# A hybrid decoder trunk on one core: a new table of slots for the second mixer's end and for the routing

## The chip, the cores and the metric

The kernel runs on one core of one Trainium2 chip. The metric is the device time of one launch in microseconds (us), the median of three runs. A profiled execution of the same program gives the trace; its times are of that one execution.

## What is computed

Two residual layers on a stream x of 256 tokens by 1024 features, all in float32. The tokens are handled as two blocks of 128.

```python
for layer in range(2):
    hn = rmsnorm(h, attn_norm[layer])
    h = h + (pool_attention_mixer(hn, ...) if layer == 0 else ssd_mixer(hn, ...))
    h = h + peer_ffn(rmsnorm(h, ffn_norm[layer]), ...)

def block(xb):                                   # peer_ffn, for 128 tokens
    q = (xb @ w_q).reshape(n, 8, 2, 128)
    s = einsum('nhie,ike->nhik', q, keys)
    top_s, top_i = top_k(s, 16)                  # then the 16 best of the 16 x 16 sums
    gate = softmax(best_s)
    act = gelu(einsum('nhkd,nd->nhk', expert_u[idx], xb))
    return einsum('nhk,nhkd->nd', gate * act, expert_v[idx])
```

Each token thus picks 8 heads x 16 = 128 of 16384 experts, each with one row of u and one of v, 4 KiB each. Gathering these rows is most of the data that is moved: 2 layers x 2 blocks x 128 picks x 1 MiB.

## The kernel before

The kernel goes through four phases (layer 0 block 0, layer 0 block 1, layer 1 block 0, layer 1 block 1) of 128 slots. In a slot, one pick of each of the 128 tokens is handled. POOL gathers u and v of the 128 rows (1 MiB, line 437) into one of ten places of `ring`; VectorE multiplies u by hn and sums it (`dot`, line 1305); ScalarE takes the gelu (line 907); VectorE multiplies by the gate (`coefs`, line 1313); ScalarE makes a diagonal matrix of each coefficient (line 914); TensorE multiplies it with v and adds up in `acc` (line 752). The last four go by pairs of slots. POOL issues the gather of a slot ten slots on only when the pair that used its place has been summed on TensorE (`pairs_summed`).

Beside these slots, every engine works in its own program order on the mixer and the queries of the *next* phase (`side`), and on the routing of the heads (`route`: top 16, candidates, expert numbers, gate). Each of these is a Python generator that yields *ticks*; each engine runs its steps up to the tick that `pace(phase, n)` gives for slot n. `pace` interpolates linearly between the `KNOTS`, which come from the table `SIDE_SLOTS`. In the second mixer `T_IN1` begins the input projection, `T_CB` and `T_SCAN` the chunked scan, `T_YT` the transposes of y, `T_OUT1` the output projection (four weight chunks of 2 MiB, 16 ticks), whose two halves VectorE adds to h in `add_to_stream` (an operation recorded at line 963, `h<-h,dve_bank`); at `T_END1` VectorE does the norm for the queries (`prepare`), and from `T_END1 + T_Q` each head's queries take four ticks. The side program of a phase starts at slot 4 (`FIRST_SIDE`) of the phase before (14 in phase 0). So table slot 81, say, is slot 85 of the phase. In slots 2 and 3 of phases 1 to 3, VectorE adds the sums of the phase before to h (`add_even`, `add_odd`), and at slot 4 begins the next norm. TensorE's pair sums stand two slots behind in its program (it sums the pair 2, 3 while VectorE is meant to be at slot 5).

SyncE loads the weight chunks into two buffers, each as soon as TensorE has used the last one. The routing of a head has four parts, at the slots in `ROUTE_DUE`: part 0 the top 16 of both score rows, part 1 the candidates, part 2 the expert numbers (after which POOL may gather for the head), part 3 the gate.

In this, the order on each engine is fixed when the program is built: an engine that waits holds up everything behind it.

Of the kernel before, what the change touches and what calls it, by code (L numbers as in the profile page):

```python
# [13 lines left out]
NBLK = SEQ // P  # L14
# [16 lines left out]
PH, NK, HALF, TOPK = 8, 128, 128, 16  # L31
# [5 lines left out]
SLOTS = PH * TOPK  # L37
# [25 lines left out]
T_SCAN = T_CB + 6  # L63
T_YT = T_SCAN + 30
T_OUT1 = T_YT + 4
T_END1 = T_OUT1 + 16 + 1
T_END = (T_END0, T_END1)
T_Q, T_PART = 3, 4
T_QUERIES = T_Q + T_PART * PH
# [3 lines left out]
START = [0]  # L73
for _phase in range(PHASES):
# [1 line left out]
EARLY_HEADS = 4  # L76
T_EARLY = T_END0 + T_Q + T_PART * EARLY_HEADS - 1
QUERIED_BY = 14
ASKED_BY = 121

HALF_P = P // 2
AHEAD = RING // GROUP
# [3 lines left out]
    ((0, 0.5), (3, 1), (5, 2), (6, T_IN0), (32, T_IN0 + 16), (56, T_OUT0), (70, T_OUT0 + 8), (72, T_END0),  # L86
     (74, T_END0 + 1), (76, T_END0 + 2), (77, T_END0 + T_Q)),
    ((0, 0.5), (3, 1), (5, 2), (6, T_IN1 - 2), (9, T_IN1 - 1), (10, T_IN1), (40, T_IN1 + 32), (46, T_CB), (51, T_SCAN),
     (73, T_YT), (76, T_YT + 1), (77, T_YT + 2), (80, T_YT + 3), (81, T_OUT1), (93, T_OUT1 + 16), (94, T_END1),
     (96, T_END1 + 1), (98, T_END1 + 2), (99, T_END1 + T_Q)),  # L90
)
FIRST_SIDE = GROUP + 2
KNOTS = [(0, T_EARLY + 1), (QUERIED_BY - 1, START[1])]
for _phase in range(1, PHASES):
    _from = (_phase - 1) * SLOTS + (QUERIED_BY if _phase == 1 else FIRST_SIDE)
    for _slot, _tick in SIDE_SLOTS[_phase // NBLK]:
        KNOTS.append((_from + _slot, START[_phase] + _tick))
    KNOTS.append(((_phase - 1) * SLOTS + ASKED_BY, START[_phase + 1]))
    KNOTS.append((_phase * SLOTS, START[_phase + 1]))


ROUTE_PARTS = 4
ROUTE_LEAD, ROUTE_STEP = 20, 3
ROUTE_DUE = []
for _phase in range(PHASES):
    for _head in range(PH):
# [45 lines left out]
def build_trunk(nc, io):  # L152
# [6 lines left out]
    with ctx:  # L159
# [193 lines left out]
        def pace(phase, n):  # L353

            return float(np.interp(phase * SLOTS + n, *zip(*KNOTS)))

        def routes_due(phase, n):

            return sum(due <= phase * SLOTS + n for due in ROUTE_DUE) - 1

        def one_after_another(side):

            for phase in range(PHASES):
                yield START[phase] + 0.5
                for tick in side(*divmod(phase, NBLK)):
                    yield START[phase] + tick
# [416 lines left out]
        def _(act):  # L783
# [120 lines left out]
            def take_gelu(g, q):  # L904
                cols = slice(q * GROUP, (q + 1) * GROUP)
                act.wait_ge(sem("dot_done"), g * BODY + (q + 1) * GROUP)
                act.activation(acts[:, cols], dots[:, cols], ACT.Gelu).then_inc(sem("gelu_done"), 1)  # L907

            def make_diagonals(g, q):
                act.wait_ge(sem("coef_done"), g * GROUPS + (q + 1))  # L910
                for rows in range(2):
                    act.wait_ge(sem(f"pairs_summed{rows}"), g * GROUPS + (q + 1 + AHEAD - DIAGS // GROUP))
                for s in range(GROUP):
                    ins = act.activation(diag[:, (q * GROUP + s) % DIAGS], folded, ACT.Copy,  # L914
                                         scale=coefs[:, q * GROUP + s:q * GROUP + s + 1])
                ins.then_inc(sem("diag_ready"), 1)
# [14 lines left out]
            def experts(phase, beside, routes):  # L931
                first = phase * STEPS
                for n in range(SLOTS):
                    g, q = first + n // BODY, n % BODY // GROUP
                    if n % GROUP == GROUP - 1:
                        take_gelu(g, q)
                    if n >= FIRST_SIDE or not phase:
                        beside.upto(pace(phase, n))
                    routes.upto(routes_due(phase, n))
                    if n % GROUP == GROUP - 1:  # L940
                        make_diagonals(g, q)
                    if n == GROUP - 1 and phase:
                        copy_odd(phase - 1)
# [4 lines left out]
            beside, routes = Side(one_after_another(side)), Side(all_routes(route))  # L948
# [9 lines left out]
        def _(dve):  # L958
# [121 lines left out]
            def mixer1(b):  # L1080
# [122 lines left out]
                    tt(yT[:, 4 * c:4 * c + 4], banks_in.take().rearrange("p (k t) -> p k t", k=4),  # L1203
                       gate_gain[:, 4 * c:4 * c + 4].unsqueeze(2).to_broadcast([P, 4, P]), name="dve_emptied")
                for n in range(2):
                    yield T_OUT1 + 8 * n + 8
                    add_to_stream(b, n, banks_in.take(), "dve_emptied")

            def top16(*rows):
# [137 lines left out]
            def experts(phase, beside, routes):  # L1347
                first = phase * STEPS
                for n in range(SLOTS):
                    g = first + n // BODY  # L1350
                    dot(phase, g, n % BODY)
                    if n == GROUP and phase:
                        add_even(phase - 1)
                    if n == GROUP + 1 and phase:
                        add_odd(phase - 1)
                        if phase == PHASES - 1:
                            lane.tell("out_ready")
                    if n >= FIRST_SIDE or not phase:
                        beside.upto(pace(phase, n))
                    routes.upto(routes_due(phase, n))  # L1360
                    if n % GROUP == GROUP - 1:
                        coefficients(phase, g, n % BODY // GROUP)

            dve.wait_ge(sem("x_loaded0"), 16)
            beside, routes = Side(one_after_another(side)), Side(all_routes(route))
# [58 lines left out]
```

## Time and profile before

| what | value |
|---|---|
| median of three runs | 1685.33 us (1685.25 to 1685.48) |
| the profiled execution | 1688.61 us |
| its span in the trace | 1686.8 us |
| TensorE matmul, VectorE, ScalarE, POOL busy | 1200.5, 1186.6, 496.0, 579.5 us |
| moved by the DMA engines | 670.19 MB, mean 397 GB/s |
| expert gathers, weight chunks | 512 of 1 MiB, 60 of 2 MiB |

Phase 0 starts near 106 us, phase 1 near 498, phase 2 near 930, phase 3 near 1353 us of the span (the first dots of each). Busy time of TensorE is modelled and overlaps; GB/s is what the core's 16 DMA engines moved in a stretch. In the rows, `<-` names what an engine waited for just before the operation.

### The profile page before, as it was taken

How to read it: one execution, taken by the hardware profiler on the slowest of the kernel's cores; microseconds unless marked ns; L12 is line 12 of the kernel's file. 1: busy time of each engine (PE TensorE's matmuls, PEld its weight loads, DVE VectorE, ACT ScalarE, POOL GpSimd, SP SyncE). 2: the span in 40 equal slices, each digit the busy share in tenths (PEclk: the TensorE clock that was granted, in tenths of full speed). 3: DMA queues.
4: the chain of work that ended last, by engine and by line, in shares of the span. 5: the costliest groups of instructions: out<-in, count | busy, mean ns of one | idle time of the engine just before them, and what ended most of it. 6: DMA issues, size and time to landing. Idle time of an engine off the chain costs nothing.

```text
span 1686.8 us, 21750 instructions
## 1 busy us (share of the span) xinstructions
PE 1200.5 (71%) x7384; PEld 578.5 (34%) x7384; DVE 1186.6 (70%) x3380; ACT 496.0 (29%) x1139; POOL 579.5 (34%) x525
## 2 busy tenths in 40 slices
PE   6866876767857985886786698589687855566554
PEld 2453222224423653442253266344234511111111
DVE  3355768866568877888574888788937587777754
ACT  0121224312222543462122354255202322222211
POOL 1023423433334322323233433232323444444551
PEclk9987988888977997998999699899798977767787
DMA  8579999999999999999999999999999999999995
GB/s 306 194 290 423 422 423 421 390 424 421 423 422 406 425 422 406 367 397 386 424 415 422 412 423 423 422 418 393 372 404 387 421 422 421 422 421 421 422 420 240
DMA packets 84076, 670.19 MB, mean 397 GB/s; under 512 B 9376, under 2 KB 9520, under 8 KB 10624
## 3 DMA queue, kind: packets, MB, share of 16 engines
q0 software_dynamic: 74608, 540.65, 78.0%
q1 hardware_dynamic: 9216, 127.65, 18.2%
q8 instruction: 58, 0.95, 0.2%
q10 hardware_dynamic: 144, 0.52, 0.1%
q14 instruction: 50, 0.41, 0.1%
HBM read 667.74 MB, written 1.05 MB: 396 GB/s over the span
## 4 chain that ended last, share of the span: by engine, by line
DMA 30%; PE 28%; DVE 28%; issue 6%; ACT 6%; POOL 1%; DVEq 0%; POOLq 0%; SPq 0%; ACTq 0%; PEldq 0%
DMA ring<-in_experts,idx 28%; PE acc L752 13%; DVE ring L1305 9%; PE act_bank L494 6%; PE dve_bank L480 5%; DVE scratch L963 3%; DMA wbuf<-in_weights 3%; ACT L788 2%; DVE onehot L963 2%; DVE scratch L1119 1%; ACT diag L914 1%; POOL ring L437 1%; ACT scratch L788 1%; PE act_bank L480 1%; PE act_bank L733 1%
## 5 line engine op out<-in xcount | busy, mean ns | idle before, releaser
L437 POOL DMA_INDIRECT ring<-in_experts,idx x512 | 573.4, 1120 | 1060.0 <-PE acc L752 864.3
L752 PE MATMUL acc<-ring,diag 64*64 64x512 f32 x4096 | 624.4, 738 | 377.5 <-ACT diag L914 366.6
L1305 DVE CUSTOM_DVE_ANT_0 ring<-ring,hn 128x1024 f32<-128x1024 f32 x512 | 621.3, 1223 | 227.5 <-DMA ring<-in_experts,idx 210.7
L752 PEld LDWEIGHTS acc<-ring,diag 64*64 64x64 f32 x4096 | 156.1, 156 | 744.7 <-ACT diag L914 497.8
L494 PEld LDWEIGHTS act_bank<-hnT,wbuf 128*128 128x128 f32 x2048 | 238.9, 194 | 63.6 <-issue 62.0
L494 PE MATMUL act_bank<-hnT,wbuf 128*128 128x128 f32 x2048 | 253.0, 281 | 10.8 <-ACT scratch L788 9.6
L907 ACT ACTIVATE acts<-dots 128x2 f32<-128x2 f32 x256 | 52.0, 203 | 709.3 <-DVE dots L1305 708.1
L914 ACT ACTIVATE diag<-cst,coefs 128x64 f32<-128x64 f32 x512 | 150.3, 340 | 262.8 <-DVE coefs L1313 250.6
L788 ACT ACT_TABLE_LOAD x80 | 102.6, 1283 | 11.7 <-DMA rowc<-in_rows 9.2
L1313 DVE TENSOR_TENSOR coefs<-acts,gate 128x2 f32<-128x2 f32 x256 | 41.3, 161 | 87.6 <-ACT acts L907 78.7
L480 PE MATMUL dve_bank<-wbuf,scratch 128*128 128x512 f32 x192 | 93.7, 627 | 8.6 <-DMA wbuf<-in_weights 7.3
L907 ACT ACT_TABLE_LOAD x68 | 87.2, 1283 | 7.3 <-DVE dots L1305 1.2
L788 ACT ACTIVATE scratch<-act_bank 128x512 f32<-128x512 f32 (+2 forms) x94 | 48.0, 511 | 132.6 <-PE act_bank L494 80.1
L681 PE MATMUL act_bank<-wbuf,hnT 128*128 128x512 f32 x128 | 59.0, 598 | 0.0
L480 PEld LDWEIGHTS dve_bank<-wbuf,scratch 128*128 128x128 f32 x192 | 35.3, 197 | 68.5 <-issue 62.9
L963 DVE TENSOR_TENSOR h<-h,dve_bank 128x512 f32<-128x512 f32 x8 | 5.5, 688 | 67.9 <-PE dve_bank L480 67.9
L1119 DVE SCALAR_TENSOR_TENSOR scratch<-scratch,colc 128x128 f32<-128x128 f32 x192 | 53.1, 346 | 0.0
L733 PE MATMUL act_bank<-keysT,scratch 128*128 128x128 f32 x128 | 23.5, 310 | 34.8 <-issue 26.4
L1305 DVE DVE_READ_ACCUMULATOR2_ANT dots<- 128x1 f32 x512 | 42.3, 83 | 0.0
L963 DVE TENSOR_TENSOR scratch<-scratch 128x512 f32<-128x512 f32 (+3 forms) x45 | 34.8, 774 | 10.2 <-ACTq L316 7.4
L480 PE MATMUL act_bank<-wbuf,hnT 128*128 128x512 f32 x64 | 33.8, 670 | 4.6 <-DMA wbuf<-in_weights 4.0
L480 PE MATMUL dve_bank<-wbuf,hnT 128*128 128x512 f32 x64 | 32.7, 654 | 3.7 <-DVE hnT L963 2.4
(128 smaller groups left out, 823.4 us busy)
## 6 DMA issues: line engine op xcount, KB each, us to landing
wbuf<-in_weights SPq DMA_DIRECT2D x60, 2048.0 KB, 11.9
ring<-in_experts,idx POOLq DMA_INDIRECT x512, 15.6
scratch<-in_bias POOLq DMA_DIRECT2D x1, 1024.0 KB, 11.3
out<-h SPq DMA_DIRECT2D x2, 512.0 KB, 5.3
scratch<-in_bands POOLq DMA_DIRECT2D x1, 768.0 KB, 6.5
h<-in_x SPq DMA_DIRECT2D x1, 512.0 KB, 4.4
gains<-in_gains POOLq DMA_DIRECT2D x1, 512.0 KB, 4.6
h<-in_x POOLq DMA_DIRECT2D x1, 512.0 KB, 17.5
```

What stands on the lines that cost most here:

```text
L437: pool.indirect_dma_start(ring[:, n % RING], None, io[f"experts{layer}"], bass.IndirectOffsetOnAxis(idx[:, at:at + 1], 0),).then_inc(sem(f ...
L480: ins = pe.matmul(out[:, 0:cols], lhsT[:, k], w[:, k], start=first and k == 0, stop=last and k == KD - 1)
L494: ins = pe.matmul(out[:, n * P:(n + 1) * P], w[:, k, j * P:(j + 1) * P], hnT[:, k], start=k == 0, stop=k == KD - 1)
L681: ins = pe.matmul(out_z, hnT[:, k], w[:, k], start=k == 0, stop=k == KD - 1)
L752: last[rows] = pe.matmul(acc[rows][half][home:home + HALF_P], diag[part, n % DIAGS], ring[part, slot, D + half * CW:D + (half + 1) * CW], ...
L788: lane(act.activation(out, in_, func, **more), name)
L907: act.activation(acts[:, cols], dots[:, cols], ACT.Gelu).then_inc(sem("gelu_done"), 1)
L914: ins = act.activation(diag[:, (q * GROUP + s) % DIAGS], folded, ACT.Copy, scale=coefs[:, q * GROUP + s:q * GROUP + s + 1])
L963: lane(dve.tensor_tensor(out, in0, in1, op), name)
L1119: done = lane.start(dve.scalar_tensor_tensor(out, tiles[:, j, tap:tap + P], taps[:, t, tap:tap + 1], out, ALU.mult, ALU.add))
L1305: dve.tensor_tensor_reduce(out=ring[:, slot, 0:D], in0=ring[:, slot, 0:D], in1=hn[:, phase % NBLK], scale=1.0, scalar=0.0, op0=ALU.mult, o ...
L1313: dve.tensor_tensor(coefs[:, cols], acts[:, cols], gate[:, bass.ds(at, GROUP)], ALU.mult).then_inc(sem("coef_done"), 1)
```

## The change

The table of slots is changed in four places, and nothing else: no operation is added or taken away.

1. The second mixer's output product takes 15 slots in place of 12, the scan's last steps and the transposes stand up to one slot from where they were, and each half of the product is added to h three ticks later (`T_OUT1 + 8n + 11`). `T_END1` is three ticks later to fit; in slots the norm for the queries moves from 94 to 101 of the table, the first query from 99 to 106.
2. The last queries are asked by other slots (`LAST_ASKED`): those for phase 2 by slot 132, four slots into phase 2; those for phase 3 two heads by slot 118 of phase 2, and the other six spread up to slot 80 of phase 3.
3. A head's routing begins 14 slots ahead of its first slot in place of 20, with 2 slots between its four parts in place of 3.
4. ScalarE and VectorE may do side steps in the first four slots of a phase too.

```diff
-T_END1 = T_OUT1 + 16 + 1
+T_END1 = T_OUT1 + 16 + 4
...
-ASKED_BY = 121
...
-     (73, T_YT), (76, T_YT + 1), (77, T_YT + 2), (80, T_YT + 3), (81, T_OUT1), (93, T_OUT1 + 16), (94, T_END1),
-     (96, T_END1 + 1), (98, T_END1 + 2), (99, T_END1 + T_Q)),
+     (70, T_SCAN + 27), (72, T_SCAN + 29), (74, T_YT), (77, T_YT + 1), (78, T_YT + 2), (81, T_YT + 3), (82, T_OUT1),
+     (97, T_OUT1 + 16), (101, T_END1), (103, T_END1 + 1), (105, T_END1 + 2), (106, T_END1 + T_Q)),
 )
+LAST_ASKED = {1: ((121, PH),), 2: ((SLOTS + 4, PH),), 3: ((118, 2), (SLOTS + 80, PH))}
...
-    KNOTS.append(((_phase - 1) * SLOTS + ASKED_BY, START[_phase + 1]))
-    KNOTS.append((_phase * SLOTS, START[_phase + 1]))
+    for _slot, _heads in LAST_ASKED[_phase]:
+        KNOTS.append(((_phase - 1) * SLOTS + _slot, START[_phase] + T_END[_phase // NBLK] + T_Q + T_PART * _heads))
...
-ROUTE_LEAD, ROUTE_STEP = 20, 3
+ROUTE_LEAD, ROUTE_STEP = 14, 2
...
-                    if n >= FIRST_SIDE or not phase:
-                        beside.upto(pace(phase, n))
+                    beside.upto(pace(phase, n))
...
-                    yield T_OUT1 + 8 * n + 8
+                    yield T_OUT1 + 8 * n + 11
```

The guard is taken out on ScalarE and on VectorE alike; TensorE had none.

## Rows read from the trace of the kernel before

**Rows 1.** The page, transfers in 40 equal slices of the span, GB/s.

```profile
GB/s 306 194 290 423 422 423 421 390 424 421 423 422 406 425 422 406 367 397 386 424 415 422 412 423 423 422 418 393 372 404 387 421 422 421 422 421 421 422 420 240
```

**Rows 2.** Windows by phase: busy us of each engine, PEclk, DMA share, GB/s.

```profile
120.00:500.00 380.00, 271.34 (x1624) 119.28 (x1627) 264.73 (x742) 100.19 (x263) 137.95 (x126) 0.85 1.01 419
500.00:927.00 427.00, 330.06 (x2184) 180.77 (x2176) 317.04 (x920) 153.98 (x314) 138.60 (x126) 0.91 0.99 407
927.00:1353.00 426.00, 331.82 (x2192) 181.46 (x2188) 328.80 (x958) 153.03 (x314) 141.55 (x130) 0.90 0.99 408
1353.00:1665.00 312.00, 175.29 (x996) 43.29 (x1000) 219.22 (x591) 71.41 (x213) 145.31 (x121) 0.75 1.01 421
```

**Rows 3.** Who waited for whom: us in total, times, longest us.

```profile
DVE h L963 <- PE dve_bank L480: 67.9, 7, 13.7
```

**Rows 4.** Timeline of VectorE: start us, us, operation, idle before and its releaser.

```profile
833.55 0.69 DVE L963 TENSOR_TENSOR h<-h,dve_bank 128x512 f32<-128x512 f32 x1 [9.84 <-PE dve_bank L480]
...
1239.70 0.69 DVE L963 TENSOR_TENSOR h<-h,dve_bank 128x512 f32<-128x512 f32 x1 [13.75 <-PE dve_bank L480]
...
1266.16 0.69 DVE L963 TENSOR_TENSOR h<-h,dve_bank 128x512 f32<-128x512 f32 x1 [12.85 <-PE dve_bank L480]
```

**Rows 5.** Windows around the output product of phases 1 and 2, columns as above.

```profile
780.00:860.00 80.00, 61.83 (x303) 24.33 (x296) 50.30 (x134) 15.15 (x44) 26.42 (x24) 0.89 1.00 407
1210.00:1300.00 90.00, 70.64 (x352) 30.18 (x352) 54.43 (x157) 16.61 (x50) 25.87 (x26) 0.89 0.97 394
```

**Rows 6.** Timeline of TensorE in the output product of phase 2.

```profile
1214.41 3.69 PE L752 MATMUL acc<-ring,diag 64*64 64x512 f32 x16 [4.55 <-ACT diag L914]
...
1222.68 1.95 PE L752 MATMUL acc<-ring,diag 64*64 64x512 f32 x16
1224.56 5.80 PE L480 MATMUL dve_bank<-wbuf,scratch 128*128 128x512 f32 x12
```

**Rows 7.** Timeline of VectorE: a landing awaited; first and following instruction of routing parts.

```profile
501.10 1.23 DVE L1305 CUSTOM_DVE_ANT_0 ring<-ring,hn 128x1024 f32<-128x1024 f32 x1 [0.68 <-DMA ring<-in_experts,idx]
...
505.23 0.17 DVE L1255 TENSOR_SCALAR pos_hi<-best_pos 128x16 uint32<-128x16 uint32 x1
...
509.00 1.23 DVE L1305 CUSTOM_DVE_ANT_0 ring<-ring,hn 128x1024 f32<-128x1024 f32 x1 [0.19 <-DVE idx L1274]
...
518.25 0.17 DVE L1292 TENSOR_REDUCE stat<-expd 128x1 f32<-128x16 f32 x1
...
518.93 0.16 DVE L1313 TENSOR_TENSOR coefs<-acts,gate 128x2 f32<-128x2 f32 x1
...
1241.64 0.48 DVE L1213 MAX8 top_s<-scores 128x8 f32<-128x128 f32 x2
...
1244.26 1.23 DVE L1305 CUSTOM_DVE_ANT_0 ring<-ring,hn 128x1024 f32<-128x1024 f32 x1 [0.18 <-DVE top_i L1217]
...
1248.13 0.29 DVE L1246 TENSOR_TENSOR cand<-top_s 128x128 f32<-128x128 f32 x1
...
1250.86 0.16 DVE L1313 TENSOR_TENSOR coefs<-acts,gate 128x2 f32<-128x2 f32 x1
```

**Rows 8.** Timeline of POOL: gathers (the first of each pair).

```profile
524.31 0.94 POOL L437 DMA_INDIRECT ring<-in_experts,idx  x1 [4.82 <-PE acc L752]
...
527.39 1.65 POOL L437 DMA_INDIRECT ring<-in_experts,idx  x1 [0.89 <-PE acc L752]
...
531.17 0.94 POOL L437 DMA_INDIRECT ring<-in_experts,idx  x1 [0.56 <-issue]
...
1204.13 0.94 POOL L437 DMA_INDIRECT ring<-in_experts,idx  x1 [9.45 <-PE acc L752]
```

**Rows 9.** Windows of 5 us where the transfers dip, columns as above.

```profile
525.00:530.00 5.00, 5.00 (x48) 2.83 (x44) 4.66 (x12) 1.38 (x5) 3.50 (x4) 1.00 0.87 329
955.00:960.00 5.00, 5.00 (x35) 2.16 (x28) 4.43 (x8) 1.15 (x5) 1.88 (x2) 0.77 0.95 362
1200.00:1205.00 5.00, 4.53 (x28) 1.01 (x24) 4.61 (x18) 0.79 (x3) 0.87 (x1) 0.70 0.49 205
```

More of the change, by code:

```diff
@@ L1357, in experts @@
                             lane.tell("out_ready")
-                    if n >= FIRST_SIDE or not phase:
-                        beside.upto(pace(phase, n))
+                    beside.upto(pace(phase, n))
                     routes.upto(routes_due(phase, n))
```

## The prediction, made before the changed kernel was run

> **What bounds the kernel now.** I read the page first, its line of GB/s above all. From the fourth slice on the transfers run at about 422 GB/s, with dips [rows 1]; no compute engine is near full, TensorE busy 330 and VectorE 317 of the 427 us of phase 1 [rows 2]. So the DMA engines bound the kernel, and a compute engine counts only where it lets them run dry. The second view is the windows by phase [rows 2]. Against the 421 of the last phase, taken as 422 at full flow, the lost time is 380 x 3/422 = 2.7 us in phase 0, 427 x 15/422 = 15.2 in phase 1, 426 x 14/422 = 14.0 in phase 2, and 312 x 1/422 = 0.7 in phase 3: 32.6 us between 120 and 1665. The bytes are the same after the change, and the start and the tail are untouched, so no version of this table can give more than about 33 us, and each part is to be priced as dry time of the DMA engines.
>
> A slot's gather is 1 MiB, 1.049 MB / 422 GB/s = 2.49 us; a pair of slots takes 4.98, and so, nearly, does a 2 MiB weight chunk (4.97). The ring holds ten slots: the gather of slot n+10 is issued when TensorE has summed slot n. A late VectorE or TensorE is thus free until the queue of gathers is empty.
>
> The third view is who waits: VectorE waits 67.9 us, 7 times, for the output product before it adds it to h [rows 3]. Two such waits stand in each block of the second mixer, four in all, three of which are shown, of 9.8 to 13.75 us [rows 4]. They are at slots 91 and 97 of phases 1 and 2. But 50 us of waits aren't 50 us of time: the windows around them show what they and the late norm behind them cost, 80 x 15/422 = 2.8 us in phase 1 and 90 x 28/422 = 6.0 us in phase 2 [rows 5].
>
> **The change, part by part.** *Output of the second mixer and the end.* The four chunks of the output product are spread over 15 slots in place of 12, and each half's add comes three ticks later. TensorE's work: 12 matmuls take 5.80 us, so a chunk of 16 takes 7.7 and four take 31; a pair's sum takes 1.9 at full clock [rows 6]. In 12 slots that is 31 + 6 x 1.9 = 42 us, while the gathers of 12 slots take 30 and the two or three chunks that load meanwhile take 10 to 15: TensorE is level with the supply or behind it. In 15 slots it is 31 + 7.5 x 1.9 = 45 against 37 + 15 = 52. The first add came 6 slots after the product's first tick, with TensorE finished at 5.3 slots plus the two by which its sums trail; now it comes 10.3 slots after it, with TensorE at 6.6 plus two. The wait should go from 13 us to nearly none. The norm behind it moves from slot 98, where it stood beside the stall and the third part of a routing, to 105. What is recovered lies between 0 and 8.8 us (2.8 + 6.0); I take 8.0, since the sums above leave TensorE room and nothing else is late there. What is late next is the first routing of the next block, due at slot 114, one slot after ScalarE's copy of its scores; were it missed, VectorE would wait about a slot, 2.5 us, under a queue of gathers.
>
> *Routing 14 slots ahead, in steps of 2.* Nothing is added; the four parts of each head move from slots 12, 15, 2 and 5 (modulo 16) to 2, 4, 6 and 8. They take VectorE 2.6 us (part 0), 2.7 (part 1), 3.8 (part 2) and 0.7 (part 3) [rows 7]. Indices come out at the slot whose number is 8 below the head's first; gathers run at most ten ahead of the sums, and slot 7's pair is coefficients and a sum later than part 2 at slot 6, so POOL gets no new wait. The cost lies at the start of phases 1 and 2. There VectorE does the adds of the last phase (slots 2 and 3) and the next norm (slots 4 and 5). In slots 0 to 2 VectorE is level with the landings (it waits 0.68 us for one at 501.10 [rows 7]), and still will be. Counted from there, route work done before: 3.8 by slot 3, 4.5 by slot 5, and no more to slot 9. After: 2.6, 5.3, 9.1 by slot 7, 9.8 by slot 9. So the sums of slots 4/5, 6/7 and 8/9 come 0.9, 4.6 and 5.3 us later. Before, the gathers they release start at 524.31, 527.39 and 531.17 [rows 8], and the DMA engines run partly dry just then (5 x (1 - 329/422) = 1.1 us in one window) [rows 9]. After: 525.2, 532.0, 536.5. The first costs 0.9; the next gap is 6.8 where one pair feeds only 4.98, which costs 1.8 to 1.9; the next gap, 4.5, costs nothing. That is 2.8 us. In phase 2 the pattern repeats with a dip of 0.7 us [rows 9]; I take 2.8 again, 5.6 in all. Phase 3 has no norm there and showed no dry time; I take 0, with 5.3 as the other end.
>
> *Scan of the second mixer.* Its steps move by at most one slot. Dry time there comes from VectorE's sum of work up to slot 77: the gather that ends the largest gap (2.6 us in one window) starts at 1204.13, right after the pair 76/77 [rows 8, 9]. From slot 42 to 77 it does 22.2 us of routing before (nine parts) and 19.6 after (eight): a gain of 2.6, if it enters slot 42 no later. It enters later, by up to 5.3 us, as the parts of slots 34 to 40 come later; waits for landings there swallow some of it. Per block that is +2.6 to -2.7; I take +0.5, 1.0 in all.
>
> *Phase 0.* Only the routings move. Its 2.7 us of dry time fall where the first mixer's attention and output meet routing parts, now out of slots 60 and 63. Between -1 and +2.7; I take 1.0.
>
> *Queries.* Six heads of the last block go to phase 3, slots 0 to 80, and phase 1's end runs to slot 132. The bytes are the same; TensorE is busy 175 of 312 us in phase 3 and VectorE 219 [rows 2]. The queries of a head come some 17 slots ahead of its routing. Nothing, then; without that cover, a head late by a slot would cost 2.5. Letting side steps run in slots 0 to 3 touches just these queries: 0.
>
> Sum: 8.0 + 1.0 + 1.0 - 5.6 + 0 = 4.4 us less. The profiled execution took 1688.6 (span 1686.8 and 1.8 around it), and would take 1684.2; the median of the runs is 3.3 lower, 1685.3, and so 1680.9.
>
> **The rivals.** (1) *The stalls were cover.* Half the loss around them stays, because TensorE's sums, not VectorE, set the gathers' pace there: 4.0 in place of 8.0, thus 1684.9. For it: 13 us waits cost only 2.8 us in phase 1. Against: the spreading helps TensorE too. (2) *Packed routing costs more than the output gives.* All three phase starts lose the whole 5.3 us: 16 us, against 10.0 of gains: 1691.3, slower. It decides where the gather released by slots 6/7 starts over 4.98 us after the one before it with an empty queue. For it: phases 1 and 2 were already at that edge. Against: the ring has cover in phase 3, and the parts formerly at slots 124 and 127 are gone. (3) *The scan gains as well.* If VectorE enters slot 42 on time and half the 15.2 + 14.0 of phases 1 and 2 goes: 14.6 + 1 - 5.6 = 10.0 less, 1675.3. (4) *TensorE cools in the thinned product.* The 16 matmuls of a sum sometimes take 3.69 us in place of 1.95 [rows 6], which I read as the lower of the two levels, 1.2 GHz; a chunk would go from 7.7 to some 14.6, the block's stretch from 45 to 86 against a supply of 52. The gathers would fall short by up to 34 us in each of two blocks; if half of that came true, 1685.3 + 34 is about 1719. But TensorE would then be busy throughout, and busy stretches here hold the full clock. The Trainium skill, TensorE: Matmul & The Clock Gate, section "HAM oscillation — how this bites in real kernels", has thinly fed TensorE falling back to half rate; the mean clock of 0.75 in phase 3, where TensorE is least busy, agrees [rows 2].
>
> **How the numbers follow.** Forecast 0.49, its own range 1677 to 1682. Rival 1: 0.26. Rival 2: 0.13. Rival 3: 0.10. Rival 4: 0.02. Two tenths of a per cent are 3.4 us, about what a measurement of this kernel can tell from no change: faster means under 1681.9. The forecast and rival 3 give faster 0.59, rival 1 same, 0.26, rivals 2 and 4 slower, 0.15. The range from 1673.0 to 1688.0 leaves out rivals 2 and 4 and the far end of rival 3, just under 2 in 10.
>
> **What would show it.** Right: VectorE's waits before h<-h,dve_bank at slots near 97 and 104 under 4 us; about 420 GB/s through that stretch in phases 1 and 2. Right on the cost: some 30 us after the starts of phases 1 and 2 the GB/s dip by 2 to 3 us more each than the 1.1 and 0.7 of before. Wrong: gather gaps in the output stretch stay at 6 us and more (rival 1); phase 3 below 421 GB/s at its start (rival 2); no gap near slot 86 of phase 2 (rival 3). The whole is wrong if dry time appears at a place not named here, such as slots 66 to 77, where routing now meets the scan.

## The result, and the profile after

The changed kernel was slower: median 1692.0 us of five runs (1688.6 to 1694.7) beside 1685.3 for the kernel before, run on the same chip; the ratio is 1.0035, 95% interval 1.0021 to 1.0049. A second series of 12 runs gave 1691.8 and 1.0029 [1.0016, 1.0043]. Forecast was 1680.9, with 1673 to 1688 as the range. Ratios here come with their 95% intervals; they differ by up to 0.0015 (in e1) from the plain quotient of the medians.

The profiled execution of the changed kernel took 1688.6 us, the fastest of its five, and that of the kernel before 1688.6 too, 3.3 above its median. So the two traces can show where time moves, but their totals don't show the difference; that comes from the runs. Part of it is the start: the first dot of phase 0 stands at 106.4 us of the span before, and at 102.8 in the changed kernel, 3.6 us earlier (104.2 in the trace of its second series).

The first view is the page's line of transfers in 40 slices, beside [rows 1]:

```profile
GB/s 306 199 315 422 425 420 409 401 422 421 423 422 380 423 424 422 352 414 363 426 419 422 417 424 424 421 380 413 327 424 422 421 421 423 421 420 422 421 421 241
```

Slices are 42.2 us. Slices 30 and 31, where the output product of phase 2 stands, are full (424 and 422; before 404 and 387). Dips have become deeper at slice 13 (406 to 380, the start of phase 1), 17 (367 to 352), 19 (386 to 363), 27 (418 to 380) and 29 (372 to 327). Slices 3 (290 to 315), 18 (397 to 414) and 28 (393 to 413) are fuller, partly because a phase now starts 5 to 11 us earlier in the span, so that the same slice holds other slots. The same in windows, columns as in [rows 2]:

```profile
500.00:545.00 45.00, 30.71 (x206) 14.93 (x207) 39.53 (x125) 13.41 (x32) 17.89 (x14) 0.78 0.97 382
925.00:975.00 50.00, 34.82 (x226) 21.73 (x225) 39.39 (x113) 18.29 (x43) 17.31 (x16) 0.80 1.01 417
690.00:705.00 15.00, 14.69 (x71) 7.26 (x64) 10.20 (x27) 9.85 (x14) 4.03 (x4) 0.89 0.66 234
755.00:775.00 20.00, 12.58 (x76) 4.75 (x76) 17.67 (x42) 5.43 (x15) 6.97 (x6) 0.74 0.78 289
1120.00:1135.00 15.00, 12.99 (x67) 7.38 (x67) 10.75 (x25) 9.85 (x14) 4.88 (x4) 1.00 0.80 304
1175.00:1210.00 35.00, 20.96 (x116) 8.32 (x116) 31.14 (x76) 10.21 (x22) 11.06 (x9) 0.80 0.79 295
780.00:860.00 80.00, 56.14 (x248) 18.18 (x248) 53.51 (x157) 15.04 (x42) 28.22 (x25) 0.85 1.01 423
1210.00:1300.00 90.00, 67.75 (x311) 23.14 (x312) 62.76 (x182) 18.41 (x52) 30.11 (x30) 0.83 1.01 423
1353.00:1665.00 312.00, 185.25 (x1156) 63.91 (x1156) 218.92 (x609) 71.69 (x217) 145.07 (x118) 0.81 1.01 421
```

- The two output windows are at 423, where they were at 407 and 394 [rows 5].
- The end of the scan is where the time went: 1175 to 1210 at 295 GB/s is 35 x (1 - 295/422) = 10.5 us of lost flow. The same windows of the kernel before, for phase 2:

```profile
1120.00:1135.00 15.00, 14.34 (x75) 7.33 (x76) 13.13 (x43) 10.77 (x17) 4.91 (x5) 1.00 1.02 419
1175.00:1210.00 35.00, 23.40 (x138) 9.41 (x137) 32.65 (x96) 12.91 (x26) 13.92 (x12) 0.80 0.86 345
```

Before it was 35 x (1 - 345/422) = 6.4 there. VectorE is busy 31.1 of the 35 us (32.7 before), while the transfers are far from full: in this stretch the DMA engines wait for the compute engines.

Who waits, columns as in [rows 3]:

```profile
DVE ring L1304 <- DMA ring<-in_experts,idx: 267.5, 191, 7.3
DVE h L962 <- PE dve_bank L480: 17.3, 2, 10.6
DVE scratch L1152 <- PE dve_bank L652: 5.9, 3, 2.6
DVE scratch L962 <- PE dve_bank L664: 3.0, 2, 2.3
```

Of the 67.9 us before `h`, 17.3 are left, all in the first mixer: the four waits of the second mixer are gone. VectorE waits for landings instead (267.5 us in the first line, 210.7 before), which costs nothing while the transfers are at full flow. The last two lines are the scan's own (decay product and group product on TensorE, awaited by VectorE); the kernel before had 2.7 and 1.0 there.

POOL's gathers at the end of the scan of phase 2, beside the last row of [rows 8]:

```profile
1189.15 1.20 POOL L437 DMA_INDIRECT ring<-in_experts,idx  x1 [11.14 <-PE acc L752]
...
1193.99 1.29 POOL L437 DMA_INDIRECT ring<-in_experts,idx  x1 [1.53 <-PE acc L752]
...
1205.43 0.94 POOL L437 DMA_INDIRECT ring<-in_experts,idx  x1 [8.17 <-PE acc L752]
```

Two gaps, of 11.1 and 8.2 us, where a pair of slots feeds the engines for 5; before there was one such gap, of 9.45. What VectorE does in them is the timeline of some of its work there (the dots between are left out):

```profile
1152.15 0.42 DVE L962 TENSOR_TENSOR scratch<-dve_bank,scratch 128x256 f32<-128x256 f32 x1 [2.27 <-PE dve_bank L664]
...
1154.74 2.36 DVE L962 TENSOR_TENSOR scratch<-scratch 128x512 f32<-128x512 f32 x3
...
1157.86 0.49 DVE L1212 MAX8 top_s<-scores 128x8 f32<-128x128 f32 x2
...
1174.42 2.37 DVE L962 TENSOR_TENSOR scratch<-scratch 128x512 f32<-128x512 f32 x3 [0.32 <-ACTq L316]
...
1177.54 0.17 DVE L1254 TENSOR_SCALAR pos_hi<-best_pos 128x16 uint32<-128x16 uint32 x1
```

A scan group's arithmetic (in the first case a wait of 2.27, then 2.36 for its three wide operations) and a routing part stand close together: part 0 at 1157.86, part 2 at 1177.54.

**Dry time by slots.** Windows in us don't follow the same work from kernel to kernel, so I also counted by slots: the time between the dots of two slots, less the bytes moved meanwhile over 422.5 GB/s. In each column the first number is phase 1, the second phase 2, in us; the last column is the median of the runs. It is arithmetic on the traces, one execution each, good to about 1 us an entry; e12 is the changed kernel a second time, e15 is e5 a second time, and the other labels are explained below.

```
slots             0-14      14-42     42-60     60-80      80-104    104-128    sum  median
before            1.7  1.0  -0.1 -0.1  4.4  0.2  5.2  4.1  3.5  6.9  0.8  2.7   30.2  1685.3
changed           2.7  0.0   1.4  0.4  3.9  1.0  8.8 12.9  1.1  0.5  0.2  0.4   33.3  1692.0
e12_changed       2.5  0.0   1.3  0.2  2.0  1.1  8.4 14.5  1.2  0.9  0.2  0.3   32.6  1691.8
e1_route_only     3.6  4.1   1.3  0.9  3.8  0.4  5.9  8.0  0.6  3.6  0.2  0.4   32.6  1688.0
e2_heads_back     1.6  0.1  -0.2  0.0  4.7  1.8  8.2 10.5  3.0  2.4  0.2  0.3   32.7  1688.7
e3_old_scan       2.5  0.1   1.1  0.3  3.1  0.1  4.4  7.0  2.8  3.7  0.1  0.1   25.3  1684.4
e5_output_only    3.1  0.3  -0.2 -0.1  4.9  2.0  4.7  3.0  2.7  4.4 -0.1  0.2   24.8  1681.6
e15_output_again  1.4  0.1  -0.1 -0.1  4.6  1.8  4.7  4.9  2.4  4.4  0.1  0.2   24.4  1683.7
e6_norm_early     3.2  0.0   0.2  1.2  1.8  0.5  4.7 11.5  0.9  2.2  0.1  0.3   26.7  1685.2
e7_squeezed       3.4  0.1   0.1  0.0  1.6  1.3  6.0 11.8  3.6  3.0  0.1  0.3   31.1  1690.3
e8_add_late       1.2  1.7   0.0 -0.2  5.1  0.4  6.2  3.7  2.9  6.2  0.0  0.2   27.3  1684.2
e14_packed_early  0.2  0.1   0.0  0.2  5.6  4.0  4.1  3.5  4.6  5.4  0.1  0.3   28.2  1688.4
```

Slots 80 to 128 fell from 13.9 to 2.1 us, 11.8 less, more than the 8.0 forecast for the output. Not all of it is the output's: without its edit, e1 has 4.7 there, 9.2 less than before, and with its edit alone e15 has 7.1, 6.8 less. Slots 60 to 80 rose from 9.3 to 21.7, 12.4 more, 10.3 of it in slots 74 to 80 (1.9 to 12.2).

### The profile page after: what moved, and what is told of

The parts are those of the page before. It is cut to its first block, busy times and chain, and to the rows that moved or that the text cites. A ratio compares the mean times of both kernels' runs of the same rounds, so it can differ in the third digit from the quotient of the medians.

```text
span 1686.8 us, 21747 instructions
## 1 busy us (share of the span) xinstructions
PE 1203.2 (71%) x7384; PEld 591.5 (35%) x7384; DVE 1191.1 (71%) x3380; ACT 489.5 (29%) x1135; POOL 602.0 (36%) x525
## 4 chain that ended last, share of the span: by engine, by line
DVE 33%; DMA 29%; PE 24%; issue 6%; ACT 4%; POOL 1%; DVEq 0%; POOLq 0%; SPq 0%; ACTq 0%; PEldq 0%
DMA ring<-in_experts,idx 27%; DVE ring L1304 12%; PE acc L752 10%; PE act_bank L494 6%; PE dve_bank L480 4%; DVE scratch L962 3%; DMA wbuf<-in_weights 3%; DVE onehot L962 2%; POOL ring L437 1%; ACT L788 1%; PE act_bank L681 1%; DVE scratch L1118 1%; PE act_bank L480 1%; ACT scratch L788 1%; ACT diag L914 1%
## 5 line engine op out<-in xcount | busy, mean ns | idle before, releaser
L437 POOL DMA_INDIRECT ring<-in_experts,idx x512 | 596.0, 1164 | 1037.7 <-PE acc L752 851.0
L752 PE MATMUL acc<-ring,diag 64*64 64x512 f32 x4096 | 603.5, 714 | 358.6 <-ACT diag L914 343.1
L1304 DVE CUSTOM_DVE_ANT_0 ring<-ring,hn 128x1024 f32<-128x1024 f32 x512 | 624.6, 1224 | 287.4 <-DMA ring<-in_experts,idx 267.5
L752 PEld LDWEIGHTS acc<-ring,diag 64*64 64x64 f32 x4096 | 151.5, 151 | 690.2 <-ACT diag L914 448.9
L494 PE MATMUL act_bank<-hnT,wbuf 128*128 128x128 f32 x2048 | 268.2, 290 | 21.9 <-ACT scratch L788 13.9
L494 PEld LDWEIGHTS act_bank<-hnT,wbuf 128*128 128x128 f32 x2048 | 252.3, 203 | 86.5 <-issue 79.2
L733 PE MATMUL act_bank<-keysT,scratch 128*128 128x128 f32 x128 | 25.3, 327 | 39.7 <-issue 34.6
L733 PEld LDWEIGHTS act_bank<-keysT,scratch 128*128 128x128 f32 x128 | 19.3, 216 | 56.7 <-issue 56.7
```

What stands on the lines that cost most here:

```text
L437: pool.indirect_dma_start(ring[:, n % RING], None, io[f"experts{layer}"], bass.IndirectOffsetOnAxis(idx[:, at:at + 1], 0),).then_inc(sem(f ...
L494: ins = pe.matmul(out[:, n * P:(n + 1) * P], w[:, k, j * P:(j + 1) * P], hnT[:, k], start=k == 0, stop=k == KD - 1)
L733: ins = pe.matmul(out[:, i * NK:(i + 1) * NK], qT[:, 2 * hd + i], keysT[:, layer, i], start=True, stop=True)
L752: last[rows] = pe.matmul(acc[rows][half][home:home + HALF_P], diag[part, n % DIAGS], ring[part, slot, D + half * CW:D + (half + 1) * CW], ...
L1304: dve.tensor_tensor_reduce(out=ring[:, slot, 0:D], in0=ring[:, slot, 0:D], in1=hn[:, phase % NBLK], scale=1.0, scalar=0.0, op0=ALU.mult, o ...
```

## The experiments

Every kernel was run beside the kernel before on the same chip, and the ratios are to that. All edits are to the changed kernel unless it says "from the kernel before".

### Which part costs

The theory: two costs that add up, the scan's moved steps (the larger) and the packed routing, against a gain at the output as forecast. The rival: a single overload at slots 60 to 80 that only the meeting of both makes, so that undoing either gives back all.

**e1_route_only**, from the kernel before:

```diff
-ROUTE_LEAD, ROUTE_STEP = 20, 3
+ROUTE_LEAD, ROUTE_STEP = 14, 2
```

> The kernel before, with only the routing changed to 14 slots ahead in steps of 2. Theory R (the routing's new place costs, because its four parts now fall on slots 66 to 72, on top of the scan of the second mixer, and on slots 2 to 8, on top of the adds and the norm): the dips at 690 to 705, 755 to 775, 1125 to 1135 and 1175 to 1210 us that the changed kernel shows are here too, and the output stretch still loses its 8.8 us: 1693 to 1701. Rival S (the scan's and the transposes' new slots, with queries in the first slots, made the dips): no new dips, 1684 to 1688.

Measured: 1688.0 us, 1.0002 [0.9986, 1.0018], far below what theory R gave. The new dips of the scan are there in part (273, 401, 345 and 360 GB/s in the four scan windows above, where the changed kernel has 234, 289, 304 and 295). And the output stretch doesn't still lose its 8.8 us, though the product and the adds stand as before:

```profile
780.00:860.00 80.00, 61.14 (x290) 24.19 (x291) 53.57 (x157) 16.15 (x44) 27.10 (x24) 0.91 1.01 423
1210.00:1300.00 90.00, 70.48 (x366) 29.31 (x363) 60.27 (x179) 18.25 (x51) 30.88 (x28) 0.91 0.99 408
```

The four waits before `h` fell from 49.7 to 30.2 us. So the routing edit alone moves dry time rather than adding much: by the slots 7.3 us more up to slot 42, 4.2 more from 42 to 80, 9.2 less from 80 on. The start of phase 2, for which the changed kernel is at 417 and the kernel before at 414:

```profile
925.00:975.00 50.00, 30.33 (x183) 11.59 (x179) 40.85 (x113) 16.56 (x39) 19.46 (x16) 0.73 0.95 379
```

That is 50 x (414 - 379)/422 = 4.1 us more there (3.1 by the slots 0 to 14 in the count, and 1.9 in phase 1). The phase-start loss exists in both phases. In the changed kernel phase 2's is absent. My reading is that a weight chunk fills the hole, since its last queries now run to slot 132; no run changes that alone. SyncE's timeline of the changed kernel has two loads between 905 and 960 us, 23.7 us from the first's issue to the end of the second's, thus the second near 940:

```profile
916.82 23.68 SPq L385 DMA_DIRECT2D wbuf<-in_weights  x2
```

The kernel before and e1 have one load there, at 905.50 and 906.01.

**e2_heads_back**, routing of all heads but the first as before. (The first head of a phase can't go back to 20 slots ahead: its top 16 would stand at slot 108 of the phase before, and its queries are asked from slot 110. That wasn't tried.)

```diff
-            _due = _phase * SLOTS + _head * TOPK - ROUTE_LEAD + _part * ROUTE_STEP
+            _due = _phase * SLOTS + _head * TOPK - (20 - 3 * _part if _head else ROUTE_LEAD - _part * ROUTE_STEP)
```

> The changed kernel, with the old routing (20 ahead, steps of 3) for heads 1 to 7; only head 0 of each block keeps 14 ahead in steps of 2, as its scores aren't there earlier. Theory R: the output product's gain stays and the scan's dips go back to the size of before: 1674 to 1681, faster than both kernels. Rival S: the dips stay, 1689 to 1694.

Measured: 1688.7, 1.0012 [1.0000, 1.0024]: not faster than both kernels, so theory R missed, and the dips of slots 60 to 80 stayed (18.7 us).

**e3_old_scan**, the scan's steps as before, everything behind it as changed:

```diff
-     (70, T_SCAN + 27), (72, T_SCAN + 29), (74, T_YT), (77, T_YT + 1), ...
+     (73, T_YT), (77, T_YT + 1), ...
```

> The changed kernel, with the scan's ticks up to the transposes spread evenly over slots 51 to 73 as before (the transposes and the output keep their new slots). Theory R: the sum of VectorE's work up to slot 77 is the same, so within 3 us of the changed kernel, 1689 to 1695. Rival S: the dips at 1175 to 1210 shrink by half or more, 1680 to 1686.

Measured: 1684.4, 0.9994 [0.9976, 1.0013], as rival S had it. Three of the windows shown above:

```profile
755.00:775.00 20.00, 13.91 (x90) 5.33 (x93) 18.82 (x45) 5.50 (x16) 8.55 (x9) 0.83 1.00 412
1120.00:1135.00 15.00, 14.85 (x79) 7.47 (x78) 10.78 (x26) 10.52 (x15) 5.13 (x5) 1.00 0.88 346
1175.00:1210.00 35.00, 23.04 (x140) 8.76 (x143) 32.46 (x86) 11.69 (x26) 15.23 (x13) 0.90 0.95 360
```

They were 289, 304 and 295. One edit of three knots moves these by (412 - 289) x 20/422 = 5.8, 1.5 and 35 x 65/422 = 5.4 us. By the slots, 60 to 80 has 11.4 us in place of 21.7.

**e4_no_spread**, all the last queries by slot 4 of phase 3:

```diff
-LAST_ASKED = {..., 3: ((118, 2), (SLOTS + 80, PH))}
+LAST_ASKED = {..., 3: ((SLOTS + 4, PH),)}
```

> The changed kernel, with the last block's queries not spread over the last phase but asked by slot 4 of it, as the phase before does. Theory R: nothing but the place of one 2 MiB weight load changes, 1690 to 1694. A rival that blames the last phase (queries late, a cooler TensorE): 1684 to 1688, and GB/s of the last phase goes up from its 421.

Measured: 1692.7, 1.0043 [1.0029, 1.0058], beside 1.0035 and 1.0029 of the changed kernel. By the middle values the place of the last block's queries is worth 1.3 or 2.4 us, and the intervals overlap: no effect that these runs show.

**e5_output_only** has the edits of e2 and e3 together; **e15_output_again** is the same kernel a second time.

> The changed kernel with both the old scan spacing and the old routing of heads 1 to 7, that is, the output product's room, the late adds and the spread queries alone. Theory T (three parts that add up: the output gives about 9 us back, the scan's new spacing costs about 7, the routing's new place about 3): 1692 - 7.6 - 3.3 = 1681, between 1678 and 1683. Rival U (time that VectorE doesn't lose at the output is lost at the scan in any case, since transfers only run dry later): 1684 to 1688.

> The kernel of e5_output_only again, beside the other two on one chip: 1680 to 1683 and faster than the kernel before by 0.2 to 0.4 per cent.

Measured: 1681.6, 0.9967 [0.9953, 0.9981], of six runs; again, of eleven, 1683.7, 0.9980 [0.9969, 0.9990]. This is the version that beats both kernels, as theory T had it.

What follows, in ratios (means of the two series where there are two):

```
                   routing 14 / 2       routing as before
scan as changed    1.0032 (changed)     1.0012 (e2)
scan as before     0.9994 (e3)          0.9974 (e5, e15)
```

The scan's knots cost 0.0038 in the one column and 0.0038 in the other, 6.4 us; the packed routing 0.0020 in both rows, 3.4 us; what is left is -0.0026, 4.5 us less. These two effects add, and the single overload falls: undoing either gives back only its own share. The intervals are 0.0010 to 0.0018 to each side, so a difference of two ratios is known to some 0.002. The scan's cost is clear of that, the routing's isn't, and with the output as before (e1) it is 0.0002. By the quotients of the medians the scan costs 0.0041 and 0.0040, the routing 0.0016 and 0.0015 (0.0017 in e1), and what is left is -0.0020, 3.3 us less: the same picture, with less at the output. The dry time agrees on the scan (7.6 us in the one column, 8.1 in the other, by the means of the traces) and shows only 0.3 and 0.7 us for the routing. Whether output and routing add as well isn't shown. The count speaks against it: both edits clear slots 80 to 128, where e1 has 4.7 us and e15 7.1 of the 13.9, and what one has cleared the other can't gain.

### Why the scan's knots cost 6 us

The old line from (51, `T_SCAN`) to (73, `T_YT`) does 1.36 ticks a slot, and so reaches tick 27 after 19.8 slots. The new knots do 27 ticks in 19 slots, 1.42 a slot, then slow down: ticks 27 to 30 come by slot 70, 71, 72 and 74. Two things are mixed in that: the squeezed steps, and the early normalization behind tick 29. One run has each alone.

**e6_norm_early**, the old rate up to tick 27, then early:

```diff
-     (70, T_SCAN + 27), (72, T_SCAN + 29), (74, T_YT), ...
+     (70.8, T_SCAN + 27), (71, T_SCAN + 28), (72, T_SCAN + 29), (74, T_YT), ...
```

> The changed kernel, scan steps at their old slots, only y's normalization (ticks 28 and 29, 5.7 us of VectorE) one slot earlier, at 75 and 76 as in the change. Theory V (the scan's cost comes from rounding of the squeezed ticks to slots: VectorE's group sum falls into the slot of TensorE's product that it needs, three waits of 2 to 3 us a block): near the old spacing, 1683 to 1687. Rival W (the cost is the normalization, which is now due before the pair of slots 74 and 75 can be summed): 1689 to 1693.

Measured: 1685.2, 0.9999 [0.9987, 1.0010]: 0.0005 above e3, 0.8 us, within the noise, and as theory V had it. One entry speaks against it: its slots 60 to 80 of phase 2 are 11.5 us dry (7.0 in e3), though phase 1 has 4.7 (4.4), its slots 80 to 128 are 3.2 us less dry, and the sum over all slots is 26.7 (25.3).

**e7_squeezed**, the new rate up to tick 27, then late:

```diff
-     (70, T_SCAN + 27), (72, T_SCAN + 29), (74, T_YT), ...
+     (70, T_SCAN + 27), (71.5, T_SCAN + 28), (72.25, T_SCAN + 29), (74, T_YT), ...
```

> The reverse: the changed kernel's squeezed scan steps, with the normalization at its old slots 76 and 77. Theory V: 1689 to 1693, with VectorE's waits for the group products at slots 62 to 65 as in the changed kernel. Rival W: 1683 to 1687.

Measured: 1690.3, 1.0025 [1.0016, 1.0035], which is 0.0031 above e3, 5.2 us, and 0.0026 above e6, which ran on the same chip; those two intervals lie apart. Its waits in the scan:

```profile
DVE scratch L1152 <- PE dve_bank L652: 7.4, 3, 4.1
DVE scratch L962 <- PE dve_bank L664: 3.0, 2, 2.3
```

and those of e3_old_scan:

```profile
DVE scratch L962 <- PE dve_bank L664: 2.3, 1, 2.3
DVE scratch L1152 <- PE dve_bank L652: 2.2, 2, 1.2
```

So the squeeze is the cause, and the normalization little or nothing: that much the runs show. By what way 0.8 slot less over 27 ticks costs 6 us, they don't.

Theory V says: by rounding. `pace` cuts the ticks to whole slots, and where TensorE's product and VectorE's step that needs it come to share a slot, VectorE waits. Ticks 13 and 14 both fall in slot 65, where the old line has 65 and 66, and there VectorE waits the 2.27 us shown above (1152.15). But the old line has such pairs too, and e3 has the same wait four slots earlier, in slot 61, where ticks 7 and 8 meet:

```profile
1131.28 0.42 DVE L962 TENSOR_TENSOR scratch<-dve_bank,scratch 128x256 f32<-128x256 f32 x1 [2.27 <-PE dve_bank L664]
```

Written out for a block, the old line puts TensorE's product and VectorE's step in one slot 4 times, the new one 5 times; of ScalarE's exponential and VectorE's use of it both have 2 such pairs. The waits for the two products rose by 8.9 - 4.5 = 4.4 us from e3 to the changed kernel, in both blocks together, most of it in waits for the decay product (5.9 after 2.2). With the routing as before they rise far less, to 5.1 us in e2 from 3.0 in e5 and 3.9 in e15, and yet the knots cost the same 0.0038 there. So waits inside a slot are a part of the cost at most.

Elapsed on VectorE from the dot of slot 42 to that of slot 78, waits included, are 134.5 and 132.1 us in phases 1 and 2 of the kernel before, 132.8 and 133.4 in e3, 138.1 and 138.6 in the changed kernel, but 133.8 and 139.1 in its second trace. What the traces with the squeeze have in common is the place of the dry time: slots 74 to 80 of both blocks are 12.2, 12.1, 7.1 and 6.7 us dry in the changed kernel, its second trace, e7 and e2, and 1.9, 1.1, 0.8 and 1.8 in the kernel before, e1, e3 and e15 (e6, with the normalization alone early, has 3.4). Which steps make it stays open.

**e10_aligned**, from e5, knots meant to put each group's steps in slots without such a meeting:

```diff
-     (73, T_YT), (77, T_YT + 1), ...
+     (69, T_SCAN + 27), (71, T_SCAN + 28), (72.3, T_SCAN + 29), (73.3, T_YT), (77, T_YT + 1), ...
```

> Output room alone, with the scan at exactly three ticks in two slots, so that TensorE's product of a group and VectorE's step that needs it never share a slot, and two slots each for the last steps and the normalization. The scan is denser than in the changed kernel (18 slots for 27 ticks against 19). If rounding is the cause and not density, the waits for group products vanish and it stays at e5_output_only or better: 1677 to 1683. If density is the cause: over 1686.

Measured: 1697.4, 1.0071 [1.0052, 1.0090], the wrong way. The waits for TensorE's two products are gone, as meant. Another wait grew; its sum, and one of its rows (columns as in [rows 4]):

```profile
DVE scratch L962 <- ACTq L316: 28.4, 17, 2.4
```

```profile
709.20 2.37 DVE L962 TENSOR_TENSOR scratch<-scratch 128x512 f32<-128x512 f32 x3 [2.00 <-ACTq L316]
```

7.4 us of this wait in e5 became 28.4: my knots put ScalarE's exponential and VectorE's use of it in one slot in every group, 2.0 us in each of seven groups of the first block and 1.1 in most of the second. So a step that shares the slot of its producer can be waited for at each repetition. That these 21 us are what made the kernel 16 us slower than e5 isn't shown: these knots squeeze too (27 ticks in 18 slots), and by what was expected of this run, over 1686 us speaks for density.

**e13_scan_roomy**, from e5, two slots more for the scan, and one less for the output product (14 in place of 15):

```diff
-     (73, T_YT), (77, T_YT + 1), (78, T_YT + 2), (81, T_YT + 3), (82, T_OUT1),
+     (75, T_YT), (78, T_YT + 1), (79, T_YT + 2), (82, T_YT + 3), (83, T_OUT1),
```

> Output room with old routing (as e5_output_only), and the scan up to the transposes spread over 24 slots in place of 22; the output then has 14 in place of 15. If the scan loses by VectorE's dense work and by waits inside a slot, more room there gives 2 to 5 us more: 1677 to 1680. If it is the whole of VectorE's work up to slot 78 that counts, no matter how it is spread, the later normalization gains nothing: 1681 to 1684.

Measured: 1684.7, 0.9995 [0.9985, 1.0006], beside 0.9967 and 0.9980 of e5. More room for the scan, taken from the output, gains nothing; what it would do by itself wasn't run.

### The routing, and the output by itself

**e14_packed_early**, from e5, 20 slots ahead in steps of 2: packed, but not later. The theory: the packing costs, not the place.

```diff
-... - (20 - 3 * _part if _head ...)
+... - (20 - 2 * _part if _head ...)
```

> As e5_output_only, with the routing of heads 1 to 7 begun 20 slots ahead but in steps of 2 (slots 12, 14, 0 and 2 modulo 16). If the packing costs, it loses as the changed kernel's routing does, 3 us: 1683 to 1687. If the place costs (parts on slots 4, 6 and 8, beside the norm, and on 66 to 72), it stays: 1679 to 1682.

Measured: 1688.4, 1.0018 [1.0009, 1.0027], 0.0038 or 0.0051 above the two series of e5, and above what was expected if packing costs. So this packing costs without the later place. By the slots its dry time is 28.2 us against 24.4 in e15. The two phases' entries rise in slots 42 to 60 (4.6 to 5.6 and 1.8 to 4.0) and in 80 to 104 (2.4 to 4.6 and 4.5 to 5.4), at no one place.

**e9_routing_even**, from e5, steps of 4. The theory was that even spacing at even slots lightens VectorE's heaviest slots.

```diff
-... - (20 - 3 * _part if _head ...)
+... - (20 - 4 * _part if _head ...)
```

> Output room alone (as e5_output_only), with the routing of heads 1 to 7 begun 20 slots ahead in steps of 4, thus at slots 12, 0, 4 and 8 modulo 16. If packing of the routing is what makes VectorE late (2.6, 2.7, 3.8 and 0.7 us in few slots), the wider steps gain a little more: 1677 to 1681. If the place against the adds and the norm at slots 2 to 5 counts, it is nearer the changed kernel's place and loses: 1682 to 1685.

Measured: 1693.4, 1.0044 [1.0026, 1.0062]: a miss, 12 us above e5 and 10 above e15. The scan windows of e9, then those of e15:

```profile
1105.00:1210.00 105.00, 85.61 (x455) 42.82 (x457) 90.02 (x237) 48.78 (x80) 30.81 (x28) 0.89 0.92 370
680.00:775.00 95.00, 76.70 (x412) 38.28 (x414) 79.35 (x210) 48.34 (x80) 29.68 (x26) 0.92 0.94 377
```

```profile
1105.00:1210.00 105.00, 85.33 (x480) 40.69 (x480) 94.72 (x255) 49.38 (x83) 35.93 (x31) 0.93 0.94 384
680.00:775.00 95.00, 78.44 (x440) 37.69 (x436) 81.00 (x220) 47.33 (x79) 29.18 (x27) 0.95 0.97 391
```

105 x 14/422 + 95 x 14/422 = 6.6 us of it lie in the scans. VectorE does less there (90.0 of 105 us against 94.7), so it waits more; which meetings of steps do it stays open. Together with e14 it limits what the routing runs say: of steps of 2, 3 and 4, begun 20 slots ahead, 3 is the best and both others cost. So how densely the parts stand isn't the whole cause; which slots they get seems to matter, and no run isolates which.

**e11_both** has the edits of e9 and e10.

> The last two together. If they are independent, the sum of both differences to e5_output_only (1681.6), within 2 us.

Measured: 1711.9, 1.0146 [1.0126, 1.0167]. From 0.9974 (e5, e15), the two edits cost 0.0070 and 0.0097 alone, which makes 1.0141, within the interval: they add.

**e8_add_late**, from the kernel before, only the adds and the norm later:

```diff
-T_END1 = T_OUT1 + 16 + 1
+T_END1 = T_OUT1 + 16 + 4
...
-     (93, T_OUT1 + 16), (94, T_END1), (96, T_END1 + 1), (98, T_END1 + 2), (99, T_END1 + T_Q)),
+     (93, T_OUT1 + 16), (97, T_END1), (99, T_END1 + 1), (101, T_END1 + 2), (102, T_END1 + T_Q)),
...
-                    yield T_OUT1 + 8 * n + 8
+                    yield T_OUT1 + 8 * n + 11
```

> The kernel before with one thing: the two halves of the output are added three ticks later (slots 94 and 100 in place of 91 and 97) and the norm behind them three slots later; the product itself stays in its 12 slots. If VectorE's stalls alone were the cost in the output stretch, they shrink from 13 and 13 us to under 7 each and 4 to 7 us come back: 1679 to 1682. If TensorE's sums set the pace there, 1684 to 1687.

Measured: 1684.2, 0.9983 [0.9973, 0.9993]. The stretches of the output are at 412 and 411 GB/s (before 407 and 394, changed 423). Later adds alone give 2.9 us (1.3 by the medians). The three waits before `h` that are left in the second mixer sum to 7.8 us, where four had 49.7, and the 4 to 7 us expected from their going didn't come. With 15 slots for the product as well (e5, e15) the gain is 4.5. The intervals overlap, so that the wider product adds something isn't shown.

**e12_changed** is the changed kernel once more, beside e9 to e11 on one chip.

> The changed kernel itself once more, beside the others on the same chip, since single runs of one kernel spread by several us: 1690 to 1694, and VectorE's waits for the group products again at slots 62 to 65 and 72.

Measured: 1691.8, 1.0029 [1.0016, 1.0043]. The waits for the products are there again, in slots 60, 63 and 65.

## Why the prediction was wrong, point by point

**The bound: right.** Kernels with less dry time in the count by slots are by and large the faster ones: 24.4 us and 1683.7, 25.3 and 1684.4, 31.1 and 1690.3, 33.3 and 1692.0. The kernel before (30.2 and 1685.3, its traced execution 3.3 above its median) and e14 (28.2 and 1688.4) stand off that line by some 3 us. In the prediction's sum 426 x 14/422 is 14.1, not 14.0; nothing hangs on it.

**Output and end, -8.0: the waits went as forecast, the price was too high.** The waits and the loss in [rows 5] went, to 423 GB/s. In e15 the same two windows are at 419 and 422, but its phase 2 starts 11 us earlier, so that they don't hold the same slots; by the slots from 80 on it is 13.9 - 7.1 = 6.8 us. As time of the whole kernel e5 and e15 gained 4.5 us; the 8.0 would be a ratio of 0.9953, the edge of e5's interval and outside e15's. What is left over, some 2 us, is within what one execution differs from another, and I can't place it. Rival 1 (half of the gain stays away) came near in size. Its mechanism, sums of TensorE too late for the gathers, would have left the product's stretch below full flow; in e15 the dry time left in phase 2 is in slots 80 to 84 (4.7 us), ahead of the product, which begins at slot 86. What the prediction missed is that the routing clears much of the same stretch by itself (e1).

**Scan, -0.5 a block: the step that failed.** It began "Its steps move by at most one slot" and priced only VectorE's sum of work up to slot 77, at a gain of 0.5 us a block. Measured is a loss of 3.2 us a block (e3 against the changed kernel, e5 and e15 against e2), with 2.7 as the far end of its range. The moves under one slot were put at nothing, and they are what costs: undoing them alone gives back the 6.4 us. What looks like a move of the last steps was a squeeze of the whole scan, 27 ticks in 19 slots, with steps from tick 7 on one slot early, which the table's numbers show without any trace. How the squeeze costs is known only in part (see above). The last line of the prediction had named slots 66 to 77 as the place that would overturn it; of the dry time added from 60 to 80, most lies in slots 74 to 80.

**Routing, +5.6: about right in size, by luck.** Together it is 3.4 us by the table of ratios, and that not surely. The dip at the start of phase 1 is (406 - 382) x 45/422 = 2.6 us, with 2.8 forecast, and 2.5 by the slots up to 42; in e1 both starts lose more, 3.3 and 4.0 us. In the changed kernel phase 2's start has no loss. In phase 3 there was none: 421 GB/s, as taken. Against that, two effects weren't in the sum: what the new places of the parts cost later in the phase (4.2 us in slots 42 to 80 of e1; e14 too), and what they give in slots 80 to 128 (9.2 us in e1).

**Phase 0, a gain of 1.0: not seen.** From 120 to 500 us the changed kernel moves 418 GB/s, and 419 in its second trace, after 419 before: between nothing and a loss of 0.9 us, within what one execution differs from another.

**Queries, 0: right** as far as it can be told (e4).

**Rival 2** gave 1691.3, near what was measured, by the wrong way: it needed all three starts to lose 5.3 us, and phases 2 and 3 lost nothing. A right number from a wrong mechanism. **Rival 3** (scan gains) fell. **Rival 4** (TensorE cools) fell: in the output stretches the granted clock went from 0.89 to 0.85 and 0.83 (0.83 and 0.89 in the second trace), and the transfers were full. In phase 3, which has queries to do now, it rose from 0.75 to 0.81 (0.79). Its counterargument, that busy stretches hold the full clock, isn't what every row shows: at 955 us TensorE was busy all 5.00 us at a granted clock of 0.77 [rows 9]. The Trainium skill, TensorE: Matmul & The Clock Gate, section "HAM oscillation — how this bites in real kernels", has thinly fed TensorE falling back; the traces agree with its direction in phase 3 (0.75 with 175 us of work, 0.81 with 185) and in three of the four output stretches, and in neither place did the time follow.

The sum with the measured terms is -4.5 + 6.4 + 3.4 = +5.3 us. That it comes back to the changed kernel's mean ratio, 1.0032, is built into the table; what was tested is that both columns and both rows give the same step. From the kernel before, the routing alone gave 0.0002.

## What to carry to other kernels

Where each engine runs a fixed order in slots, don't price a changed table at nothing because each step moves by under a slot. Write out, for the old and the new table, the slot of every step: that shows where the rate of steps has risen, and which producer and consumer have come to share a slot (e10 shows what that can do, 2 us in each group). Which of the two costs has to be measured. The size of a wait says little of its price: four waits of 10 to 14 us were worth 4.5 us of time, and steps shifted by under a slot cost 6.4. And undo the edits one by one, from both ends: this change of four parts held a gain, which e5 keeps, and two of the parts cleared the same stretch.

## What was not expected of the chip

The spread between executions is larger than the first runs showed. Five runs of the kernel before lay within 0.5 us; 35 of it beside e1 to e4 lay between 1680.9 and 1691.9, and 12 of e3 between 1679.2 and 1693.3. One source is in the traces: the start. From 0 to 120 us e5 moves 263 GB/s and e15, the same kernel, 255, which is 120 x 8/422 = 2.3 us, and their profiled executions took 1681.1 and 1684.2. What sets it wasn't looked into. With 11 or 12 runs of a kernel the intervals here are still 1.5 to 3 us to each side, so a difference of 3 us is at the limit of what such a series can show, and a single trace's total says little.
